# An MLP in two phases: the up projection by seven block products too, with its split outputs kept in DRAM between the phases

## The chip, the cores and the metric

The kernel runs on one core of a Trainium2 chip. The metric is device time in microseconds (us) of one launch. The kernel before takes 3120.62 us (median of 3 runs, 3118.38 to 3122.58). One profiled execution of it has a span of 3119.9 us.

## The reference

A decoder trunk of two layers over 1024 tokens of width 1024, all in float32. Layer 0 mixes by GLA linear attention and an RG-LRU, layer 1 by a gated DeltaNet. Each layer then attends to 256 memory tokens with 4 heads and applies an MLP of width 4096 with a squared ReLU. What the change touches:

```python
def sq_relu_mlp(h, w1, w2):
    return jnp.square(jax.nn.relu(h @ w1)) @ w2

def mem_cross_attn(h, mem_n, w_q, w_kv, w_o):
    q = (h @ w_q).reshape(B, T, XA_HEADS, XA_DH).astype(F32)
    kv = mem_n @ w_kv
    k = kv[..., :D_MODEL].reshape(B, M, XA_HEADS, XA_DH).astype(F32)
    v = kv[..., D_MODEL:].reshape(B, M, XA_HEADS, XA_DH).astype(F32)
    ...
```

`h` is the residual after an RMSNorm with gain. x is 1024 tokens by 1024, w1 is 1024 by 4096, w2 is 4096 by 1024.

## The kernel before

**Precision.** A float32 product is made from three fast ones. Each operand X is split into a high part (ScalarE copies it to the type fp32r, `whi`) and a low part (VectorE subtracts, `wlo`). TensorE then adds high*high, high*low and low*high into one PSUM bank. So every 128x128 block of weights costs three matmuls for each 512 tokens.

**Tiles.** Channels lie on the partitions, tokens in the free dimension, in halves of 512. The residual `hres` takes 32 KB of each partition, the split activations `act` 64 KB. Weights stream from DRAM in blocks of 512 KB through four slots (`wraw`, `whi`, `wlo`), in the order of the list that the host makes. SyncE (SP) issues these loads in that order, each after a wait until its slot is free. Each engine's instructions stand in an order written out by hand and run in that order. Semaphores tie the engines together. `plan` (functions `schedule` and `Plan`) only counts blocks and units and says which PSUM bank a unit uses and which unit must have been evacuated before.

**The MLP.** The 32 tiles of hidden channels are worked in 8 groups of 4. A group has an up projection (192 matmuls of 128x512: 4 tiles, 2 halves of the tokens, 8 tiles of the width, 3 products) and a down projection whose outputs VectorE adds to `work` (lines L1856 and L1989). In groups 0 and 7 the down projection has 192 matmuls too. In groups 1 to 6 (a hardware loop, `body(g)`) it has 168: for each of four blocks of W2 (a to d), taken as a 2x2 matrix of blocks A, and the hidden values, taken as a 2x2 matrix B (two tile pairs by two halves of the tokens), Strassen's method in Winograd's form makes seven block products in place of eight. `SUM` names the operands of each: product 1 is A11*B11, 2 is A12*B21, 3 is S4*B22, 4 is A22*T4, 5 is S1*T1, 6 is S2*T2, 7 is S3*T3. S1 to S4 are sums of blocks of A, T1 to T4 of B. `PRODUCTS` is their order: "a5" is product 5 of block a. VectorE makes the sums of the weights (L1909 to L1914) and of the hidden values (L1951 to L1976), ScalarE and VectorE split them (L1024 to L1040, L1925, L1926, L1946). TensorE's products are L2905 to L2907.

**Elsewhere.** The memory's keys and values are 16 units of 256 columns each. The values come out transposed and TensorE turns them (`value_transposes`). In the GLA stretch TensorE makes seven levels of 128x128 score blocks per chunk (L2961), VectorE selects from each with a mask (L2246, `select`), and GpSimd makes the decays (L640 to L666). At the start ScalarE issues the loads of x and then loads its table.

## Time and profile before

| | |
|---|---|
| median of 3 runs | 3120.62 us |
| span of the profiled execution | 3119.9 us |
| TensorE busy | 3059.8 us, 98% |
| VectorE busy | 1951.3 us, 63% |
| ScalarE busy | 1209.0 us, 39% |
| GpSimd busy | 165.4 us, 5% |
| DMA | 206.01 MB, mean 66 GB/s |

The profiled execution's own time is its span to within what the page shows; nothing else of that execution is timed. PE is TensorE, DVE VectorE, ACT ScalarE, POOL GpSimd, SP SyncE, and SPq or ACTq their issuing of DMAs. Busy time of an engine is time in which it executes, so overlapping matmuls count once. The duration of one matmul is longer than its share of the time, since the next one enters behind it; a rate is therefore read from starts, or from a window's length and its count. `L1234` is a line of the kernel.

### The profile page before, as it was taken

To read this page: it belongs to the slowest core of one execution; us is meant where nothing else is said; L and a number is where in the kernel's file an instruction comes from. 1 tells how busy PE (TensorE), PEld (TensorE's weight loads), DVE (VectorE), ACT (ScalarE), POOL (GpSimd) and SP (SyncE) were. 2 spreads that over 40 slices of the span, in tenths; PEclk is the share of its full clock that TensorE was granted. 3 is DMA by queue.
4 is the path that set the end of the run, shared out by engine and by line. 5 is a ranking of instruction groups with operands and counts; after the bars stand their busy time and mean duration, and the time that the engine had idled before them with its cause. 6 is when DMAs were issued, how large, how long until landed. Compare 5 with 4: busy or idle time off the path is not lost.

```text
span 3119.9 us, 46630 instructions
## 1 busy us (share of the span) xinstructions
PE 3059.8 (98%) x17630; PEld 2520.8 (81%) x17630; DVE 1951.3 (63%) x3087; ACT 1209.0 (39%) x2304; POOL 165.4 (5%) x270
## 2 busy tenths in 40 slices
PE   8999999999999999999999999999999999999997
PEld 6788898887888888887888788879888788888886
DVE  7276647547566666667555566644764756666666
ACT  3335545345332332244111366644534533333322
POOL 0019300000000000000000112100000000000000
PEclk9999999999999999999999999999999999999999
DMA  3110331012111111212222221123101211111122
GB/s 133 34 48 22 115 115 41 28 41 95 48 54 54 54 54 47 94 54 82 102 94 97 82 76 57 54 65 112 41 28 41 95 48 54 54 54 54 48 94 80
DMA packets 81321, 206.01 MB, mean 66 GB/s; under 512 B 6304, under 2 KB 39344, under 8 KB 80176
## 3 DMA queue, kind: packets, MB, share of 16 engines
q1 hardware_dynamic: 40320, 141.91, 14.0%
q10 hardware_dynamic: 40880, 62.41, 5.5%
q8 instruction: 85, 1.39, 0.2%
q14 instruction: 36, 0.29, 0.0%
HBM read 174.93 MB, written 29.36 MB: 65 GB/s over the span
## 4 chain that ended last, share of the span: by engine, by line
PE 86%; DVE 8%; ACT 3%; issue 2%; DMA 1%; ACTq 0%; DVEq 0%; SPq 0%
PE ps L2636 42%; PE ps L2652 14%; PE ps L2907 5%; PE ps L2905 5%; PE ps L2906 5%; PE ps L3071 2%; PE ps L3001 2%; DVE work L1545 1%; PE ps L3203 1%; PE ps L3076 1%; PE ps L2961 1%; DVE work L1561 1%; DVE hres L1576 1%; PE ps L3186 1%; DVE wlo L1529 1%
## 5 line engine op out<-in xcount | busy, mean ns | idle before, releaser
L2636 PE MATMUL ps<-act,whi 128*128 128x512 f32 x3664 | 1147.4, 394 | 6.7 <-DVE work L1706 2.7
L2636 PEld LDWEIGHTS ps<-act,whi 128*128 128x128 f32 x3664 | 684.3, 188 | 167.1 <-issue 12.2
L2636 PE MATMUL ps<-act,wlo 128*128 128x512 f32 x1832 | 717.1, 391 | 0.0
L1529 DVE TENSOR_TENSOR wlo<-wraw,whi 128x1024 fp32r<-128x1024 f32 x257 | 314.0, 1223 | 304.3 <-ACT whi L725 301.4
L725 ACT ACTIVATE whi<-wraw 128x1024 fp32r<-128x1024 f32 x214 | 225.5, 1056 | 570.4 <-DMA wraw<-wstream_dram 567.7
L2636 PEld LDWEIGHTS ps<-act,wlo 128*128 128x128 f32 x1832 | 343.9, 188 | 75.5
L2652 PE MATMUL ps<-act,whi 128*128 128x512 f32 x1376 | 370.7, 391 | 0.7 <-DVE work L2147 0.7
L2652 PEld LDWEIGHTS ps<-act,whi 128*128 128x128 f32 x1376 | 258.9, 188 | 57.0 <-issue 1.8
L1989 DVE TENSOR_TENSOR work<-work,ps 128x512 f32<-128x512 f32 x336 | 225.0, 684 | 103.8 <-PE ps L2907 103.8
L2652 PE MATMUL ps<-act,wlo 128*128 128x512 f32 x688 | 213.5, 391 | 0.0
L979 ACT ACTIVATE hidf<-hidf 128x512 f32<-128x512 f32 x96 | 60.8, 633 | 263.1 <-DVE hidf L1893 263.1
L2636 PE MATMUL ps<-hid,whi 128*128 128x512 f32 x512 | 160.2, 394 | 1.1 <-DVE hidf L1841 0.7
L2652 PEld LDWEIGHTS ps<-act,wlo 128*128 128x128 f32 x688 | 129.5, 188 | 27.8
L1018 ACT ACTIVATE whi<-wraw 128x1024 fp32r<-128x1024 f32 x48 | 49.2, 1049 | 186.8 <-DVE wraw L1910 186.8
L2636 PEld LDWEIGHTS ps<-hid,whi 128*128 128x128 f32 x512 | 95.9, 188 | 24.0 <-issue 2.1
L2905 PE MATMUL ps<-hid,whi 128*128 128x512 f32 x288 | 113.7, 395 | 0.0
L2907 PE MATMUL ps<-hid,wlo 128*128 128x512 f32 x288 | 113.3, 393 | 0.0
L1606 DVE SCALAR_TENSOR_TENSOR work<-work,pvec 128x1023 f32<-128x1023 f32 (+2 forms) x84 | 107.8, 1283 | 8.0 <-DVE work L1602 0.2
L2906 PE MATMUL ps<-hid,whi 128*128 128x512 f32 x288 | 112.7, 391 | 0.0
L671 POOL TENSOR_TENSOR work<-work,consts 128x512 f32<-128x512 f32 x16 | 20.4, 1273 | 1539.0 <-ACT work L1332 1539.0
L1893 DVE SCALAR_TENSOR_TENSOR hidf<-ps,work 128x512 f32<-128x512 f32 x96 | 66.2, 689 | 55.0 <-PE ps L2636 55.0
L2636 PE MATMUL ps<-hid,wlo 128*128 128x512 f32 x256 | 99.9, 390 | 0.0
(364 smaller groups left out, 4990.8 us busy)
## 6 DMA issues: line engine op xcount, KB each, us to landing
wraw<-wstream_dram SPq DMA_DIRECT2D x262, 512.0 KB, 3.6
qkvz<-work ACTq DMA_DIRECT2D x32, 512.0 KB, 2.7
work<-qkvz ACTq DMA_DIRECT2D x64, 256.0 KB, 3.3
hsave<-hres ACTq DMA_DIRECT2D x2, 4096.0 KB, 12.0
hres<-hsave ACTq DMA_DIRECT2D x2, 4096.0 KB, 12.8
hres<-xT_dram ACTq DMA_DIRECT2D x8, 512.0 KB, 11.0
hres<-xT_dram ACTq DMA_DIRECT2D x1, 4096.0 KB, 13.4
outT_dram<-hres SPq DMA_DIRECT2D x16, 256.0 KB, 2.0
```

The source lines that it names most:

```text
L725: A(whi[s][:], wraw[s][:], ACT.Copy).then_inc(w_hi, 1)
L1529: TT(wlo[s][:], wraw[s][:], whi[s][:].bitcast(F32), ALU.subtract).then_inc(w_split, 1)
L1606: ins = STT(out=out[:, back:], in0=x[:, 0:SEQ - back], scalar=w(3 - back), in1=out[:, back:], op0=ALU.mult, op1=ALU.add)
L1893: STT(out=hidf[:, t, 1, E[e]], in0=out_of(u + k), scalar=0.0, in1=uh(RSTD, e), op0=ALU.max, op1=ALU.mult).then_inc(evac, 1)
L1989: TT(uh(t, e), uh(t, e), out_of(u + 8 + i), ALU.add).then_inc(evac, 1)
L2636: last = mm(out_of(u)[:, 0:width], (wlo if hl else whi)[s][:, at:at + P], rhs(kt, xp, e), start=kt == hl == xp == 0, stop=kt == kts - 1 an ...
L2652: last = mm(out_of(u)[:, E[e]], (wlo if hl else whi)[s][:, kt * P:(kt + 1) * P], act[:, kt, xp, E[e]], start=kt == hl == xp == 0, stop=kt ...
L2905: mm(out_of(u), wh, bh, start=first, stop=False, skip_group_check=more)
L2906: mm(out_of(u), wh, bl, start=False, stop=False, skip_group_check=more)
L2907: last = mm(out_of(u), wl, bh, start=False, stop=end, skip_group_check=more)
L3001: last = mm(out_of(u), (wlo if hl else whi)[s][:, kt * P:(kt + 1) * P], act[:, kt, xp, E[c % 2]], start=kt == hl == xp == 0, stop=kt == KT ...
L3071: last = mm(out[:, (h % 4) * P:(h % 4 + 1) * P], lhs[:, h, :], rhs[:, h, :], start=start, stop=stop)
```

## The change

Both MLPs are worked in two phases.

**Up phase.** Group 0 is made as before. Group 1's up projection is made as before, but ScalarE evacuates it. The hidden tiles of groups 2 to 7 are made two at a time, in 12 pairs (`PAIRS`). For each pair the input x is the 2x2 matrix B (halves of the width by halves of the tokens) and the two weight blocks are A. The seven products of a pair, in the order 1, 5, 6, 2, 7, 3, 4, each have 12 matmuls. Products share PSUM banks: 1, 6, 7 and 4 accumulate into one bank, and ScalarE (`kept`) and VectorE (`corner`) read it between them. The four "quads" of a pair (two tiles by two halves) then get ReLU and square on ScalarE. GpSimd makes their sums T1 to T4 (`hidden_sums`), ScalarE the high parts (`part_hi`), VectorE the low ones (`part_lo`), and SP stores all seven split operands to DRAM (`store` to `hid_store`, 512 KB each). Group 0's hidden values go to `hid_first`. The norm's factor is left out of the hidden values of groups 1 to 7.

**Down phase.** Groups 1 to 7 are worked by seven products each, with operands read back from `hid_store` (`operand`) into the space of `act`, `tx` and `hres`, two groups alternating. Then GpSimd multiplies the sum by the square of the norm's factor and group 0 is added (192 matmuls).

**Engines.** The sums of the weights and of the hidden values go from VectorE to GpSimd (`weight_sums`, `hidden_sums`). All loads and stores of the MLP are issued by SP. The hardware loops over groups are gone: the program is written out.

**Elsewhere.** The memory's values are made with the memory as the stationary operand, in four full banks (96 matmuls of 512 columns for a layer, and no transposes). In the GLA stretch the seven levels are made and selected for half of the columns only. At the start SP issues the loads of x, tile 0 and the first halves of two weight blocks first, and ScalarE loads its table at once.

The core of the diff:

```diff
+UP = "1562734"
+STAGED = ("B11", "B22", "T1", "T3", "B21", "T2", "T4")
+LO_ORDER = ("B11", "B22", "B21", "T13", "T2", "T4")
...
+        for q in range(PAIRS):
+            blocks = [plan.block(ring[2 * (q % 2) + k]) for k in range(2)]
+            banks = {"1": 0, "6": 0, "7": 0, "4": 0, "5": 1, "3": 1, "2": 2}
+            for name in UP:
+                u = plan.fixed((0 if q % 2 else 4) + banks[name])
+                if name in "24":
+                    plan.after[blocks["24".index(name)]] = u
+            plan.by_hand.update(blocks)
+        here(f"mlp{layer}.d")
...
+                def store(hp, *ops):
+                    for op in ops:
+                        nth = LO_ORDER.index(op if op not in ("T1", "T3") else "T13")
+                        sp.wait_ge(hid_ready, HIDS * layer + 2 * MLP_T + len(LO_ORDER) * hp + nth + 1)
+                        sp.dma_start(hid_store[hp // 2, STAGED.index(op), :, hp % 2], stage(op).bitcast(F32)).then_inc(out_of_op(op), 16)
...
+                for q in range(PAIRS):
+                    last = q == PAIRS - 1
+                    if last:
+                        for op in ("B11", "T1", "T2"):
+                            operand(0, op)
+                    load(n + 2 * q + 4)
+                    if last:
+                        operand(0, "B21")
+                    store(q + 2, "B11", "B22")
+                    if last:
+                        operand(0, "T3")
+                        operand(0, "B22")
+                    load(n + 2 * q + 5)
+                    if last:
+                        operand(0, "T4")
+                    store(q + 2, "B21", "T1", "T3", "T2", "T4")
...
+                order = ("B11", "T1", "T2", "B21", "T3", "B22", "T4")
+                for op in order:
+                    operand(1, op)
+                n = plan.at[f"mlp{layer}.d"][0]
+                    load(n + MLP_T * i + 4)
+                    load(n + MLP_T * i + 5)
+                    more = i + 2 < MLP_G - 1
+                    for op in order:
+                        if op == "T2":
+                            load(n + MLP_T * i + 6)
+                        if more:
+                            operand(i + 2, op)
+                    load(n + MLP_T * i + 7)
...
+                def hidden_sums(hp):
+                    at = HIDDEN * layer + hp
+                    pool.wait_ge(squared, 4 * at + 3)
+                    if hp == 0:
+                        pool.wait_ge(first_out, 32 * (layer + 1))
+                    if hp:
+                        pool.wait_ge(*all_out("T1", layer, hp))
+                    tt(stage_part("T13", 1, True), quads[:, hp % 2, 1:3, :], quads[:, hp % 2, 0:2, :], ALU.subtract) \
+                        .then_inc(t_raw, 1)
+                    pool.wait_ge(t_raw, 3 * at + 1)
+                    tt(stage_part("T2", 1, True), quad(hp, "22"), stage_part("T1", 1, True), ALU.subtract).then_inc(t_raw, 1)
+                    pool.wait_ge(squared, 4 * at + 4)
+                    pool.wait_ge(t_raw, 3 * at + 2)
+                    tt(stage_part("T4", 1, True), quad(hp, "21"), stage_part("T2", 1, True), ALU.subtract).then_inc(t_raw, 1)
...
+                    k3 = link.mark(tt(s3, a11, a21, ALU.subtract))
+                    tt(a21, a21, a22, ALU.add).then_inc(w_sum, 1)
+                    link.wait(k3)
+                    k2 = link.mark(tt(s2, a22, s3, ALU.subtract))
+                    link.wait(k2)
+                    tt(s4, a12, s2, ALU.subtract).then_inc(x_sum, 1)
...
+                def kept(q, product, name):
+                    hp = q + 2
+                    uq = up_unit(layer, q, product)
+                    eng.wait_ge(t_raw, 3 * (HIDDEN * layer + hp - 1))
+                    eng.wait_ge(hid_ready, HIDS * layer + 2 * MLP_T + len(LO_ORDER) * (hp - 2) + 3)
+                    eng.wait_ge(unit_done, uq + 1)
+                    A(quad(hp, name), out_of(uq), ACT.Copy).then_inc(read_act, 1)
+                def corner(q, name):
+                    hp = q + 2
+                    eng.wait_ge(read_dve, 3 * (PAIRS * layer + q) + ("11", "22", "12").index(name) + 1)
+                    link(A(quad(hp, name), quad(hp, name), ACT.Relu))
+                    squares(hp, name)
...
+                for q in range(PAIRS):
+                    more = q + 1 < PAIRS
+                    if q:
+                        last_corner(q - 1)
+                    else:
+                        first_up(7)
+                    part_hi(q + 1, "B21")
+                    part_hi(q + 1, "T13")
+                    kept(q, "1", "11")
+                    part_hi(q + 1, "T2")
+                    if more:
+                        block_hi(blocks_of(layer, q + 1)[0])
+                    kept(q, "5", "22")
+                    part_hi(q + 1, "T4")
+                    if more:
+                        block_hi(blocks_of(layer, q + 1)[1], prep_no(layer, q + 1))
+                    else:
+                        down_hi(0, 0)
+                    kept(q, "6", "12")
+                    if more:
+                        sums_hi(prep_no(layer, q + 1), sums_of(q + 1))
+                    else:
+                        down_hi(0, 1)
+                    corner(q, "11")
+                    part_hi(q + 2, "B11")
+                    corner(q, "22")
+                    part_hi(q + 2, "B22")
+                    corner(q, "12")
+                last_corner(PAIRS - 1)
+                for op in LO_ORDER[2:]:
+                    part_hi(PAIRS + 1, op)
...
+                def part_lo(hp, op):
+                    at = HIDDEN * layer + hp
+                    eng.wait_ge(hid_hi, h0 + 2 * MLP_T + len(LO_ORDER) * hp + LO_ORDER.index(op) + 1)
+                    if op in ("T13", "T2"):
+                        eng.wait_ge(t_raw, 3 * at + (2 if op == "T13" else 3))
+                    src = stage_part(op, 1, True) if op[0] == "T" else quad(hp, op[1:])
+                    TT(stage_part(op, 1), src, stage_part(op, 0).bitcast(F32), ALU.subtract).then_inc(hid_ready, 1)
...
+                def corner(q, product, name):
+                    nth = ("11", "22", "12").index(name)
+                    eng.wait_ge(unit_done, up_unit(layer, q, product) + 1)
+                    eng.wait_ge(read_act, 3 * (PAIRS * layer + q) + nth + 1)
+                    TT(quad(q + 2, name), quad(q + 2, name), out_of(up_unit(layer, q, product)), ALU.add).then_inc(read_dve, 1)
...
+                for q in range(PAIRS):
+                    more = q + 1 < PAIRS
+                    x, bufs = prep_no(layer, q + 1), sums_of(q + 1)
+                    for op in LO_ORDER[2:]:
+                        part_lo(q + 1, op)
+                    if more:
+                        block_lo(blocks_of(layer, q + 1)[0], x)
+                    corner(q, "2", "11")
+                    if more:
+                        block_lo(blocks_of(layer, q + 1)[1], x)
+                    else:
+                        down_lo(0, 0)
+                    part_lo(q + 2, "B11")
+                    corner(q, "7", "22")
+                    if more:
+                        part_of_sums_lo(x, bufs, 0, "24")
+                    part_lo(q + 2, "B22")
+                    corner(q, "3", "12")
+                    if more:
+                        part_of_sums_lo(x, bufs, 1, "3")
+                    else:
+                        down_lo(0, 1)
+                def add(i, k):
+                    name = PRODUCTS[k]
...
+                for q in range(PAIRS):
+                    b0, b1 = blocks_of(layer, q)
+                    x, reads = prep_no(layer, q), 3 * (PAIRS * layer + q)
+                    for name in UP:
+                        u = up_unit(layer, q, name)
+                        if name in "152":
+                            eng.wait_ge(evac, plan.need[u] + 1)
+                        if name in "15":
+                            eng.wait_ge(w_split, (b0 if name == "1" else b1) + 1)
+                        if name in "67":
+                            eng.wait_ge(read_act, reads + (1 if name == "6" else 3))
+                            eng.wait_ge(x_split, 2 * x + (1 if name == "6" else 2))
+                        if name == "4":
+                            eng.wait_ge(read_dve, reads + 2)
+                        if q == 0 and name in "5674":
+                            eng.wait_ge(xt_ready, 8 * layer + 2 * "5674".index(name) + 2)
+                        a, op = SUM[name]
                         for k in range(4):
+                            last = multiply(out_of(u), weights(a, k, q), [moving(op, hl, k) for hl in range(2)],
+                                            k == 0 and name in "152", k == 3, name in "6734")
...
+                        if level < DIAG:
+                            half = CH >> (level + 1)
+                            new = at4.rearrange("p (a b) (n s t) -> p a (b n) s t", a=2, s=2, t=half)[:, :, :, 1, :]
+                            data = data.rearrange("p a (b s t) -> p a b s t", s=2, t=half)[:, :, :, 1, :]
+                            mask = masks[:, level, :].rearrange("p (b t) -> p b t", t=half).unsqueeze(1) \
+                                .to_broadcast(list(new.shape))
+                        else:
...
+                        for xp, hl in ((0, 0), (0, 1), (1, 0)):
+                            for k in range(2):
+                                last = mm(bank(4 + 2 * m + k), memhl[:, xp, at:at + P], (wlo if hl else whi)[s][:, E[k]],
+                                          start=kt == hl == xp == 0, stop=kt == KT - 1 and xp == 1)
+                    last.then_inc(unit_done, 1)
...
+            first_part(0, False)
+            for n in range(2):
+                first_hi(n, 0)
+            first_square(tile(hres, 0), 0)```

VectorE, in the middle of the up phase, one pair. `staged` is a low part that goes to DRAM, `wlo` that of a weight block, `xl_u` that of a weight sum, `quads<-quads,ps` is `corner`:

```order
547 L2229 TENSOR_TENSOR staged_78<-quads,staged_78 128x512 [waits hid_hi]
548 L2229 TENSOR_TENSOR staged_77<-stagedf_79,staged_77 128x2x512 [waits t_raw,hid_hi]
549 L2229 TENSOR_TENSOR staged_78<-stagedf_80,staged_78 128x512 [waits t_raw,hid_hi]
550 L2229 TENSOR_TENSOR staged_78<-stagedf_80,staged_78 128x512 [waits hid_hi]
551 L1871 TENSOR_TENSOR wlo_60<-wraw_56,whi_52 128x1024 [waits w_hi,x_sum]
552 L2236 TENSOR_TENSOR quads<-quads,ps 128x512 [waits read_act,unit_done]
553 L1871 TENSOR_TENSOR wlo_61<-wraw_57,whi_53 128x1024 [waits w_hi,x_sum]
554 L2229 TENSOR_TENSOR staged_77<-quads,staged_77 128x512 [waits hid_hi]
555 L2236 TENSOR_TENSOR quads<-quads,ps 128x512 [waits read_act,unit_done]
556 L2251 TENSOR_TENSOR xl_u_95<-xr_u_93,xh_u_91 128x1024 [waits x_hi]
557 L2229 TENSOR_TENSOR staged_77<-quads,staged_77 128x512 [waits hid_hi]
558 L2236 TENSOR_TENSOR quads<-quads,ps 128x512 [waits read_act,unit_done]
```

Nothing of this stood there before. The first read of PSUM (552) stands behind the low part of the next pair's weight block (551), which waits for `x_sum`.

GpSimd, in the same place, one pair. `stagedf` are T1 and T3, T2 and T4 of the hidden values, `xr_u` and `wraw` the sums of the weights:

```order
231 L871 TENSOR_TENSOR stagedf_79<-quads 128x2x512 [waits late_out,squared]
232 L874 TENSOR_TENSOR stagedf_80<-quads,stagedf_79 128x512 [waits t_raw]
233 L877 TENSOR_TENSOR stagedf_80<-quads,stagedf_80 128x512 [waits t_raw,squared]
234 L889 TENSOR_TENSOR xr_u_100<-wraw_58,wraw_59 128x512 [waits w_in3,w_in2]
235 L890 TENSOR_TENSOR wraw_59<-wraw_59 128x512
```

Before, GpSimd had no instruction in either MLP. `x_sum` is signalled by the second of two more instructions of this form behind 235.

SP, from the last pair into the first group of the down phase. `wraw` is a load of a weight block, the others read operands of the hidden values back:

```order
203 L744 DMA act<-hid_store 128x4x512 [waits early_out,unit_done]
204 L747 DMA act<-hid_store 128x2x512 [waits late_out,unit_done]
205 L747 DMA hresr<-hid_store 128x2x512
206 L695 DMA wraw_59<-wstream_dram 128x1024 [waits unit_done]
207 L695 DMA wraw_56<-wstream_dram 128x1024 [waits unit_done]
208 L695 DMA wraw_57<-wstream_dram 128x1024 [waits unit_done]
209 L744 DMA act<-hid_store 128x4x512 [waits early_out,unit_done]
210 L747 DMA tx<-hid_store 128x2x512 [waits late_out,unit_done]
```

Before, only weight blocks stood in this queue. Now each block stands behind operands that were issued ahead of it.

## Rows read from the trace of the kernel before

**Rows 1.** The page: busy time by engine, and the chain's shares.

```profile
PE 3059.8 (98%) x17630; PEld 2520.8 (81%) x17630; DVE 1951.3 (63%) x3087; ACT 1209.0 (39%) x2304; POOL 165.4 (5%) x270
...
PE 86%; DVE 8%; ACT 3%; issue 2%; DMA 1%; ACTq 0%; DVEq 0%; SPq 0%
```

**Rows 2.** Windows of two loop groups (up, down, up): length, busy (instructions), clock, DMA.

```profile
967.26:1011.38 44.12, 44.12 (x194) 36.24 (x193) 27.62 (x45) 18.29 (x28) 0.00 (x0) 1.00 0.20 71
1011.38:1049.93 38.55, 38.55 (x168) 31.35 (x167) 29.70 (x48) 7.86 (x12) 0.00 (x0) 1.00 0.08 27
1049.93:1094.04 44.11, 44.11 (x194) 36.24 (x193) 27.61 (x45) 18.29 (x28) 0.00 (x0) 1.00 0.22 71
```

**Rows 3.** VectorE groups: shapes, count, busy us, mean ns, idle before.

```profile
L1529 DVE TENSOR_TENSOR wlo<-wraw,whi 128x1024 fp32r<-128x1024 f32 x257 | 314.0, 1223 | 304.3 <-ACT whi L725 301.4 <-DVE work L1606 1.1
L1932 DVE TENSOR_TENSOR hid<-hidf,hid 128x512 fp32r<-128x512 f32 x72 | 49.3, 685 | 0.0
L1926 DVE TENSOR_TENSOR xl<-xr,xh 128x256 fp32r<-128x256 f32 x48 | 20.1, 419 | 0.0
```

**Rows 4.** ScalarE groups, same columns.

```profile
L725 ACT ACTIVATE whi<-wraw 128x1024 fp32r<-128x1024 f32 x214 | 225.5, 1056 | 570.4 <-DMA wraw<-wstream_dram 567.7 <-issue 2.6
L979 ACT ACTIVATE hidf<-hidf 128x512 f32<-128x512 f32 x96 | 60.8, 633 | 263.1 <-DVE hidf L1893 263.1
```

**Rows 5.** GpSimd groups, same columns.

```profile
L673 POOL TENSOR_TENSOR work<-work 128x512 f32<-128x512 f32 x16 | 20.3, 1270 | 93.3 <-PE ps L3154 93.3
L650 POOL TENSOR_TENSOR wlo<-wraw,whi 128x1024 fp32r<-128x1024 f32 x5 | 11.9, 2381 | 3.3 <-ACT whi L725 3.3
L666 POOL TENSOR_TENSOR lin<-lin,work 128x256 f32<-128x256 f32 x8 | 5.9, 735 | 0.0
```

**Rows 6.** Timeline, VectorE and GpSimd at 338 us: start, length, instruction.

```profile
337.85 2.38 POOL L650 TENSOR_TENSOR wlo<-wraw,whi 128x1024 fp32r<-128x1024 f32 x1 [1.97 <-ACT whi L725]
338.99 4.61 DVE L2296 TENSOR_TENSOR work<-work 128x512 f32<-128x512 f32 x2
340.19 2.86 POOL L701 TENSOR_TENSOR act<-work,act 128x1024 fp32r<-128x1024 f32 x1
```

**Rows 7.** Line L2296: ns min/median/max, first and last start.

```profile
L2296 DVE TENSOR_TENSOR work<-work x8: 678/684/2894, 339.0 to 349.8; 128x512 f32<-128x512 f32 x8
```

**Rows 8.** Timeline of PE: 256-column units of the memory; levels of the GLA stretch.

```profile
395.29 0.28 PE L2636 MATMUL ps<-memhl,wlo 128*128 128x256 f32 x1
395.41 0.40 PE L2636 MATMUL ps<-memhl,whi 128*128 128x256 f32 x2
395.64 0.28 PE L2636 MATMUL ps<-memhl,wlo 128*128 128x256 f32 x1
...
256.24 2.06 PE L2961 MATMUL ps<-lin 64*128 64x128 f32 x32
258.22 0.49 PE L2980 MATMUL ps<-lin 128*128 128x128 f32 x2
258.55 0.39 PE L2981 MATMUL ps<-lin 128*128 128x128 f32 x2
258.77 0.39 PE L2980 MATMUL ps<-lin 128*128 128x128 f32 x2
```

**Rows 9.** Window of the GLA stretch, columns as in Rows 2.

```profile
234.00:338.00 104.00, 102.76 (x870) 82.96 (x871) 70.43 (x117) 60.51 (x112) 92.75 (x192) 1.00 0.08 25
```

**Rows 10.** Timeline, the start.

```profile
7.59 1.28 ACT L1490 ACT_TABLE_LOAD   x1 [7.59 <-issue]
12.52 2.07 PE L2665 MATMUL ps<-act,whi 128*128 128x512 f32 x4 [12.52 <-DVE act L1589]
```

**Rows 11.** The page: DMA queues (packets, MB, share of 16 engines) and issues (to landing).

```profile
q1 hardware_dynamic: 40320, 141.91, 14.0%
q10 hardware_dynamic: 40880, 62.41, 5.5%
...
wraw<-wstream_dram SPq DMA_DIRECT2D x262, 512.0 KB, 3.6
...
hres<-hsave ACTq DMA_DIRECT2D x2, 4096.0 KB, 12.8
```

1051 lines of the change are left out of this document (577 added, 474 removed).

## The prediction

> **What bounds the kernel now.** I read the busy line and the chain first: TensorE is busy 98% of the span and the chain is 86% TensorE [rows 1]. Then the windows of two loop groups of the MLP: TensorE is busy for the whole of each, at full granted clock, while ScalarE and VectorE have room and GpSimd does nothing [rows 2]. So before the change only fewer or cheaper matmuls shorten the MLP, and the question for after is whether some other engine's order of work now takes longer than TensorE's. The last views are therefore durations by form [rows 3 to 5] and places where GpSimd and VectorE ran at once [rows 6, 7].
>
> The sum is made against the profiled execution. Its span, 3119.9 us, is 0.7 us under the median, 3120.6; I add the sum to the median. Two kernels of this time that differ by less than 0.2% (6 us) can't be told apart.
>
> **What goes on TensorE.** A down window has 168 matmuls in 38.55 us, 0.2295 us each, an up window 44.12 us [rows 2]. A pair in the new up phase has 84 matmuls, 19.3 us, so two pairs take 38.6 in place of 44.1: 5.5 us for each of 6 groups, 33 us. One more group's down projection gets seven products: 5.5 us. That is 38.7 us a layer, **-77.4 us**.
>
> Values of the memory: a layer drops 192 matmuls of 256 columns, three of which start in 0.35 us [rows 8], so 22.5 us, and 16 transposes. I price a transpose by the nearest 128-column matmuls, four in 0.44 us [rows 8], so 1.8 us. It adds 96 of 512 columns, 22.0 us. **-5 us** for both layers. Bounds: 0 (if the new order waits once for the blocks) and -8.
>
> GLA stretch: 32 level matmuls take 2.06 us [rows 8], 0.064 each; 56 of the 64 in each of 8 chunks lose half their columns, at most 14 us. But GpSimd, whose decays are not touched, is busy 92.75 of these 104 us [rows 9], which leaves at most 11. At the other end the load of weights sets the pace and nothing is gained. I take **-6 us**, the middle. Start: the first matmul is at 12.52 us, the table load at 7.59 behind the issuing of the loads of x [rows 10]. If the table is loaded at once and x tile 0 comes first, up to 8 us go; if the stream of x tiles then paces TensorE, none. **-4 us**.
>
> Sum of what goes: -92 us.
>
> **Up phase, a steady pair.** GpSimd now makes the sums. A 512-element sum takes 1.27 us (L673 in [rows 5]), back to back 1.25; a 1024-element one 2.38 (L650 in [rows 5]). One pair: T1 and T3 together 2.4, T2, T4 and four weight sums 6 x 1.25, in all 9.9 us. VectorE: two weight blocks and a 1024 weight sum, 1.14 each back to back, a 512 one 0.6, the staged low parts 5 x 0.6 and 1.14, in all about 8.1 us, all with both inputs in SBUF, and three reads of PSUM (2 us). ScalarE: about 14 us from its two forms, 1.06 and 0.63 [rows 4]. Each alone fits into 19.3.
>
> They don't run freely beside each other. At 338 us L2296, with both inputs in SBUF and 0.684 us alone, took 2.89 us at the longest [rows 7]: two of them took 4.61 us while two GpSimd instructions ran, each VectorE one ending just after a GpSimd one did, and GpSimd's second took 2.86 in place of 2.4 [rows 6]. So such an instruction waits for the whole of GpSimd's running one, and GpSimd for it. The Trainium skill, page "SBUF — State Buffer", section "Who interferes with whom", states this as a rule: a VectorE instruction with two SBUF inputs and a GpSimd one that reads SBUF exclude each other, and whichever began first keeps the port. It speaks against this change; by it the whole 18 us of both would stand in one row in every pair, and the trace agrees where the two met.
>
> The loop of waits of one pair, from the start of GpSimd's T1/T3 sum (0). GpSimd: 2.4; VectorE's low part of B21, which has waited, 0.6; T2 1.25; T4 1.25; VectorE's T1/T3 low part 1.1; first weight sum 1.25; VectorE's T2 part 0.6; second weight sum 1.25 (at 9.7); VectorE's T4 part 0.6; the last two weight sums 2.5: x_sum at 12.8. Only then may VectorE make the low part of the weight block, 1.2, and behind it in its queue read product 2's bank, 0.7. ScalarE: ReLU, square, high part of B11, 1.9. VectorE: low part of B11, then product 7's bank, 1.4 (this releases product 4 on TensorE). ScalarE the same again, 1.9; VectorE low part of B22 and product 3's bank, 1.4; ScalarE ReLU and square, 1.3. With that the last quad is ready and GpSimd starts the next pair: 9.9 us after x_sum with the short hops between. The loop is 22.65 us against TensorE's 19.3, and TensorE then waits about 3.35 us a pair, before products 7 (ScalarE's read of product 6 stands behind the second weight block, which waits for the second sum) and 4.
>
> Eleven such steps, 37 us. Ahead of them the same exclusion and the 8 sums of the inputs (8 x 2.4) delay ScalarE's queue in group 1's up projection, so that the first pair's loop starts up to 9 us late; I take 4. The last pair ends 1 us late. 42 us a layer, **+84 us**. Bounds: 11 (no exclusion, below) and 125 (both engines' 18 us in one row and nothing hidden: the loop grows by 1.7 more).
>
> **Into the down phase.** DMA: queue q1 moved 141.91 MB in 14.0% of the span, 325 GB/s, q10 62.41 MB in 5.5%, 364 [rows 11]. An operand pair of a group is 1 MB, a group 7.3 MB, about 21 us. Operands of group 1 of the phase may only be loaded as the last pair frees the space, and T4's last: it lands about 11 us after the pair's end, product a6 wants it at 8.3: 3 us. SP then issues the late stores of the last pair (2.6 MB) and seven operands of the next group (7.3 MB) ahead of the next group's first weight block. That block lands about 40 us into the group, but VectorE's queue wants its low part behind the 20th addition, at 31; TensorE runs out of banks at product d6. 11 us. **+28 us** for both layers; bounds 0 and 40.
>
> In a steady down group VectorE has 28 additions from PSUM (17 us back to back, not excluded) and 8 us of splits, GpSimd 16 sums of 256 elements (0.735 each [rows 5], 12 us) in 38.6 us: hidden by TensorE. The 9.4 MB of a group are 29 us at 325 GB/s: hidden. The 16 multiplications of the end take 20 us beside 44 us of TensorE. More instructions because loops are written out: nothing, since issuing is 2% of the chain [rows 1] (bounds -2 and +10).
>
> **The sum.** -92 + 84 + 28 = +20: 3141 us, with its own range 3115 to 3168.
>
> **Rivals.** One, not slower, and much faster: exclusion does not decide. VectorE's four staged parts (2.85 us) then run beside GpSimd and the loop is 19.8 us, 0.5 over TensorE: 11 us in all, and the late start goes. With 22 us into the down phase: 3120.6 - 92 + 33 = 3062. For it: only two instructions of full size met GpSimd in this trace. Against it: both waited. It decides wherever the loop is under about 20.5 us a pair. Chance 0.22.
>
> Two: exclusion holds, but late start and transition are hidden, because loads run ahead of my count: 3120.6 - 92 + 74 = 3103. For it: the block of 512 KB lands in 3.6 us [rows 11] and each wait is short when the queue is empty. Chance 0.15.
>
> Three: the round trip through DRAM decides. A pair moves 4.7 MB (14.5 us at 325 GB/s, 22 at 215), a group 9.4. If reading and writing in pieces of 2 KB came to 215 GB/s, a down group would take 44 us in place of 38.6: 5 x 6 x 2 = 60 more, 3200. Against it: q10, the queue with the smaller packets, is not the slower one [rows 11]. Chance 0.08.
>
> **Numbers.** The forecast has 0.55, rivals 0.22, 0.15 and 0.08. Faster by over 0.2%: rivals one and two and a corner of the forecast, 0.38. Within 0.2%: the forecast's lower edge and two's upper, 0.11. Slower: 0.51. The range must reach both sides: 3062 to 3170 leaves out rival three and half of what lies below one.
>
> **What would show it.** In the up phase windows of one pair of about 22.6 us with 84 matmuls; VectorE's lines L2229 and L1871 with durations well over 0.69 and 1.22, up to 3 us, and GpSimd's sums over 1.27; TensorE waiting for ScalarE's `kept` ahead of product 7 and for VectorE's `corner` ahead of 4. One gap of some 10 us in the first down group, behind a wait on `x_sum`. Steady down groups of 38.6 us. First matmul near 8 us. I am wrong if the pairs take 19.3 to 20 us, or if VectorE's durations don't stretch where GpSimd runs.

## The result and the profile after

The changed kernel takes 3213.7 us (median of 4 runs, 3210.2 to 3221.3) against 3120.5 before (3118.4 to 3122.6): ratio 1.030, 95% interval 1.029 to 1.031. The forecast, 3141, had the sign and not the size; the time is outside its range. The profiled execution has a span of 3211.8 us, 91.9 more than that of before.

The page of the changed kernel, busy line and shares of the chain, for [rows 1]:

```profile
PE 3031.0 (94%) x17070; PEld 2453.7 (76%) x17070; DVE 1970.8 (61%) x2817; ACT 1390.8 (43%) x2556; POOL 768.6 (24%) x722
...
PE 59%; DVE 11%; POOL 11%; ACT 7%; issue 5%; DMA 5%; SPq 0%; ACTq 0%; DVEq 0%; POOLq 0%
```

TensorE has 560 matmuls less and is the chain for 59% in place of 86%: it now waits for others. Windows show where: one pair of the up phase, down groups 2, 4 and 1 (for [rows 2]). A row has the window, its length, the busy time (instructions) of TensorE, its weight loads, VectorE, ScalarE and GpSimd, the granted clock, the DMA engines' share and GB/s.

```profile
855.55:878.20 22.65, 20.20 (x85) 15.55 (x84) 12.68 (x14) 14.29 (x21) 12.27 (x7) 1.00 0.56 209
1144.75:1183.90 39.15, 39.15 (x169) 31.39 (x168) 27.35 (x40) 6.00 (x9) 9.02 (x12) 1.00 0.58 206
1224.97:1266.72 41.75, 39.26 (x169) 31.38 (x168) 28.49 (x40) 8.00 (x12) 12.94 (x16) 1.00 0.64 228
1089.13:1144.75 55.62, 43.98 (x167) 34.84 (x168) 30.73 (x43) 12.74 (x19) 17.77 (x22) 0.85 0.93 341
```

A pair takes 22.65 us, a down group 39 to 44, the first one of layer 0 55.6 at a granted clock of 0.85 (that of layer 1 took 57.3). Durations by form, for [rows 3, 5]:

```profile
L2229 DVE TENSOR_TENSOR staged<-stagedf,staged 128x512 fp32r<-128x512 f32 x56 | 86.3, 1577 | 30.5 <-POOL stagedf L877 30.5
L2251 DVE TENSOR_TENSOR xl_u<-xr_u,xh_u 128x1024 fp32r<-128x1024 f32 x24 | 29.2, 1217 | 0.0
```
```profile
L871 POOL TENSOR_TENSOR stagedf<-quads 128x1024 f32<-128x1024 f32 x28 | 74.5, 2660 | 257.1 <-ACTq L1275 257.1
L877 POOL TENSOR_TENSOR stagedf<-quads,stagedf 128x512 f32<-128x512 f32 x28 | 61.8, 2205 | 4.0
L892 POOL TENSOR_TENSOR xr_u<-wraw,xr_u 128x512 f32<-128x512 f32 x24 | 41.2, 1719 | 0.0
```

A 512-element VectorE subtraction, 0.685 us alone, takes 1.58 where GpSimd works beside it; the split of the sums, made while GpSimd is idle, keeps its 1.22. GpSimd's 512-element ones take 1.7 and 2.2 in the mean of these two groups, in place of 1.27.

The timeline of GpSimd in one pair shows the loop as the prediction drew it, for [rows 6]. A row has start, length and instruction, and in brackets the idle time before it and what ended it:

```profile
857.68 2.41 POOL L871 TENSOR_TENSOR stagedf<-quads 128x1024 f32<-128x1024 f32 x1 [10.11 <-ACTq L1275]
...
861.93 2.35 POOL L877 TENSOR_TENSOR stagedf<-quads,stagedf 128x512 f32<-128x512 f32 x1
...
868.96 1.28 POOL L894 TENSOR_TENSOR xr_u<-wraw,xr_u 128x512 f32<-128x512 f32 x1
880.36 2.41 POOL L871 TENSOR_TENSOR stagedf<-quads 128x1024 f32<-128x1024 f32 x1 [10.12 <-ACTq L1275]
```

From the first subtraction to the end of the last sum 12.6 us (forecast 12.8), then 10.1 idle (9.9): 22.7.

Where the 72 us between the forecast's 20 over before and the measured 92 lie, by differences of such windows over both layers:

| part | forecast | measured | short by |
|---|---|---|---|
| 24 pairs over TensorE's 19.3 each | 84 | 106 (steady 68, first pairs 19, last pairs 18) | 22 |
| first down groups over 38.55 | 28 | 36 | 8 |
| down groups 2 to 7 | 0 | 27 | 27 |
| entry of the up phase | 0 | 8 | 8 |
| everything outside the MLP (start, GLA stretch, memory values) | -15 | -8 | 7 |

### The profile page after: what moved, and what is told of

It is laid out like the page before. It is cut to its first block, busy times and chain, and to the rows that moved or that the text cites. A ratio compares the mean times of both kernels' runs of the same rounds, so it can differ in the third digit from the quotient of the medians.

```text
span 3211.8 us, 44831 instructions
## 1 busy us (share of the span) xinstructions
PE 3031.0 (94%) x17070; PEld 2453.7 (76%) x17070; DVE 1970.8 (61%) x2817; ACT 1390.8 (43%) x2556; POOL 768.6 (24%) x722
## 4 chain that ended last, share of the span: by engine, by line
PE 59%; DVE 11%; POOL 11%; ACT 7%; issue 5%; DMA 5%; SPq 0%; ACTq 0%; DVEq 0%; POOLq 0%
PE ps L2944 17%; PE ps L2960 14%; PE ps L3166 4%; PE ps L3167 4%; PE ps L3168 4%; DMA wraw<-wstream_dram 4%; POOL stagedf L871 2%; PE ps L3394 2%; POOL stagedf L877 2%; POOL wraw L890 2%; PE ps L3324 2%; DVE quads L2236 1%; ACT quads L1274 1%; PE ps L3016 1%; DVE work L1887 1%
## 5 line engine op out<-in xcount | busy, mean ns | idle before, releaser
L2944 PE MATMUL ps<-act,whi 128*128 128x512 f32 x2384 | 754.0, 397 | 10.7 <-DVE wlo L1871 5.2
L2944 PEld LDWEIGHTS ps<-act,whi 128*128 128x128 f32 x2384 | 445.6, 188 | 120.5 <-issue 13.1
L1871 DVE TENSOR_TENSOR wlo<-wraw,whi 128x1024 fp32r<-128x1024 f32 x255 | 319.1, 1253 | 254.5 <-ACT whi L985 173.3
L2960 PE MATMUL ps<-act,whi 128*128 128x512 f32 x1376 | 371.0, 391 | 0.7 <-DVE work L2434 0.7
L2319 DVE TENSOR_TENSOR work<-work,ps 128x512 f32<-128x512 f32 x360 | 242.6, 684 | 160.3 <-PE ps L3168 159.1
L2960 PEld LDWEIGHTS ps<-act,whi 128*128 128x128 f32 x1376 | 259.0, 188 | 57.0 <-issue 1.8
L3166 PE MATMUL ps<-act,whi 128*128 128x512 f32 x624 | 250.8, 402 | 30.9 <-DVE quads L2236 18.0
L916 POOL TENSOR_TENSOR hres<-hres 128x1024 f32<-128x1024 f32 x16 | 42.7, 2709 | 870.4 <-ACT hres L1250 870.4
L3166 PEld LDWEIGHTS ps<-act,whi 128*128 128x128 f32 x624 | 118.3, 190 | 71.3 <-DVE quads L2236 28.0
L3167 PE MATMUL ps<-act,whi 128*128 128x512 f32 x416 | 164.3, 395 | 0.0
L3167 PE MATMUL ps<-hresr,whi 128*128 128x512 f32 x416 | 163.8, 394 | 0.0
L2229 DVE TENSOR_TENSOR staged<-stagedf,staged 128x512 fp32r<-128x512 f32 (+1 forms) x84 | 122.7, 1486 | 60.4 <-POOL stagedf L877 30.5
L2229 DVE TENSOR_TENSOR staged<-quads,staged 128x512 fp32r<-128x512 f32 x84 | 72.7, 869 | 120.8 <-ACT staged L1298 120.8
## 6 DMA issues: line engine op xcount, KB each, us to landing
wraw<-wstream_dram SPq DMA_DIRECT2D x260, 512.0 KB, 3.5
hid_store<-staged SPq DMA_DIRECT2D x196, 512.0 KB, 3.1
hresr<-hid_store SPq DMA_DIRECT2D x56, 512.0 KB, 10.3
qkvz<-work ACTq DMA_DIRECT2D x32, 512.0 KB, 2.6
tx<-hid_store SPq DMA_DIRECT2D x28, 512.0 KB, 7.7
act<-hid_store SPq DMA_DIRECT2D x28, 512.0 KB, 11.2
```

The source lines that it names most:

```text
L1871: TT(wlo[s][:], wraw[s][:], whi[s][:].bitcast(F32), ALU.subtract).then_inc(w_split, 1)
L2229: TT(stage_part(op, 1), src, stage_part(op, 0).bitcast(F32), ALU.subtract).then_inc(hid_ready, 1)
L2319: TT(uh(t, e), uh(t, e), out_of(uk), ALU.add).then_inc(evac, 1)
L2944: last = mm(out_of(u)[:, 0:width], (wlo if hl else whi)[s][:, at:at + P], rhs(kt, xp, e), start=kt == hl == xp == 0, stop=kt == kts - 1 an ...
L2960: last = mm(out_of(u)[:, E[e]], (wlo if hl else whi)[s][:, kt * P:(kt + 1) * P], act[:, kt, xp, E[e]], start=kt == hl == xp == 0, stop=kt ...
L3166: mm(out, wh, xh, start=first, stop=False, skip_group_check=more)
```

## Experiments

**e1 and e5: the exclusion by itself.** Small kernels outside the model, stages of 16 instructions.

> Not the model at all: ten stages of 16 instructions each, one after the other, on idle memory. Alone (stage 1 and 2) a VectorE subtraction of two SBUF tiles of 512 should take about 0.6 us back to back and a GpSimd one 1.25 (as in the trace of before). Theory (the two exclude each other for whole instructions when both read two SBUF tiles): side by side (stage 3) they alternate, a pair of them every 1.85 us, 30 us for 16 pairs in place of 20. With VectorE's second input in PSUM (stage 4) or its only input in PSUM (stage 5), as in the additions of the down phase, nothing stretches: 10 and 20 us. Rival (bandwidth shared, no exclusion): stage 3 takes about 20 us for GpSimd and less than 20 for VectorE, and stages 4 and 5 stretch as much as stage 3. Stages 8 to 10 add ScalarE copies and eight loads of 512 KB: if DMA or ScalarE also stretch VectorE by over 5%, the loop of the up phase has a third cause.

> Not the model: nine stages of GpSimd fills, GpSimd copies and GpSimd subtractions, alone and beside VectorE's subtractions of two SBUF tiles. Theory (what VectorE shares with GpSimd is a way of reading SBUF): a fill on GpSimd, which reads nothing, leaves VectorE's 16 subtractions at 9.7 us, and a GpSimd copy, which reads one tile, stretches them as a subtraction does (over 17 us). Rival (any GpSimd instruction that touches SBUF holds VectorE up): the fills stretch them too. With 1024-element VectorE subtractions (8 of 1.15 us) beside GpSimd's, the total is again close to the sum of both. A fill's own time is wanted for the next experiment, where it takes the place of a sum.

Timelines of e1: VectorE alone, then beside GpSimd's subtractions with two SBUF inputs, with the second input in PSUM, with its only input in PSUM, and with its only input in SBUF (a copy). GpSimd's rows follow: alone, and in the first two of these stages.

```profile
9.25 9.72 DVE L392 TENSOR_TENSOR dout<-din 128x512 f32<-128x512 f32 x16 [4.11 <-DMA ain<-xT_dram]
38.84 25.70 DVE L392 TENSOR_TENSOR dout<-din 128x512 f32<-128x512 f32 x16 [19.87 <-POOL pout L367]
65.79 9.66 DVE L394 TENSOR_TENSOR dout<-din,ps 128x512 f32<-128x512 f32 x16 [1.25 <-POOL pout L367]
85.57 9.66 DVE L396 COPY dout<-ps 128x512 f32<-128x512 f32 x16 [10.13 <-POOL pout L367]
105.32 21.44 DVE L398 COPY dout<-din 128x512 f32<-128x512 f32 x16 [10.09 <-POOL pout L367]
...
19.15 19.56 POOL L367 TENSOR_TENSOR pout<-pin 128x512 f32<-128x512 f32 x16 [18.71 <-DVE dout L392]
38.88 26.78 POOL L367 TENSOR_TENSOR pout<-pin 128x512 f32<-128x512 f32 x16 [0.17 <-POOL pout L367]
65.83 19.61 POOL L367 TENSOR_TENSOR pout<-pin 128x512 f32<-128x512 f32 x16 [0.17 <-POOL pout L367]
```

Side by side, 16 of each take 26.8 us; the sum of both alone is 29.3, free overlap would be 19.6. With one input in PSUM nothing stretches. The eight loads and ScalarE's copies beside them changed nothing: VectorE took 25.75 us in that stage, and ScalarE's 16 copies 8.43 us there and in the stage with VectorE's PSUM input. In e5 VectorE's 16 took 9.72 us beside GpSimd fills and 15.9 beside GpSimd copies (expected over 17). So the exclusion stands, for GpSimd instructions that read, and is a little milder than whole instructions in one row: 9% less than the sum.

VectorE's SBUF-to-SBUF copies, with one SBUF input, stretched as well: 21.4 us beside GpSimd, where the same copies from PSUM took 9.66 (from SBUF they were not run alone). The Trainium skill, page "SBUF — State Buffer", section "Who interferes with whom", states the rule with this exception: two SBUF inputs contend with a GpSimd instruction that reads SBUF and not with one that only writes it; at most one SBUF input does not contend, outside modes with two ports, which a copy can enter; ScalarE never waits, and DMA does not contend with a compute engine. The stages agree with it.

**e2: the wait that the table names.**

```diff
+                    kept(q, "6", "12")
                     if more:
                         block_hi(blocks_of(layer, q + 1)[1], prep_no(layer, q + 1))
                     ...
-                    kept(q, "6", "12")
```

> ScalarE's read of product 6 stands ahead of the high part of the second weight block, which waits for GpSimd's second weight sum; nothing else moves. The waits of the changed kernel show 1.3 to 1.7 us a pair of TensorE ahead of product 7 for this read. Theory A (a loop through GpSimd's sums, VectorE's read of product 2 behind x_sum and ScalarE's queue sets the pair; this gap is only slack that the loop leaves): pairs stay at 22.6 us, the gap moves to product 4, total unchanged within 5 us. Rival B (each gap is its own cost): pairs of about 21.3 us, 24 of them, 30 us less.

3215.9 us, the same as the changed kernel within its spread; pairs of 24.3, 21.2 and 22.7 in turn, 22.7 in the mean. Theory A: the wait ahead of product 7 is gone, the one ahead of product 4 grew from 0.86 to 1.5 and 2.5 us, and the loop stayed. The forecast of pairs at 22.6 holds for their mean only.

**e3: the loop opened.** VectorE's order in a pair, condensed to names (ScalarE's was moved likewise, and in the last pair both engines' first splits for the down phase stand behind the pair; each kind of instruction keeps its own order):

```diff
-    part_lo B21, T13, T2, T4; block_lo 0; corner 2; block_lo 1; part_lo B11; corner 7; sums 24; part_lo B22; corner 3; sums 3
+    part_lo B21, T13, T2; corner 2; part_lo T4; corner 7; block_lo 0; part_lo B11; block_lo 1; corner 3; sums 24; part_lo B22; sums 3
```

> The same instructions in the up loop in another order: VectorE reads product 2 (and 7) ahead of the low parts of the weight blocks, which wait for x_sum, and ScalarE takes product 6 and the rectifying of product 2 ahead of the sums' high parts. GpSimd is untouched. Theory A (exclusion stretches a loop of waits that closes through x_sum; the engines have 18 us of excluded work for 19.3 us): with the read of product 2 out of the loop pairs fall from 22.65 to 19.3 to 20 us, 11 x 2 x 3 = 60 to 70 us less in all, though VectorE and GpSimd still wait for each other instruction by instruction. Rival B (the 18 us of both in one row are themselves the bound, or DMA is): the order gives little, pairs stay above 22, under 10 us less.

3146.5 us, 67 less; ratio to before 1.0076 (1.0059 to 1.0093). A window of one pair, and two of VectorE's rows in the next:

```profile
854.42:873.83 19.41, 19.41 (x85) 15.78 (x84) 16.35 (x14) 13.99 (x22) 12.24 (x7) 1.00 0.66 244
```
```profile
874.53 2.89 DVE L2250 TENSOR_TENSOR xl_u<-xr_u,xh_u 128x512 fp32r<-128x512 f32 x1
877.34 1.78 DVE L2228 TENSOR_TENSOR staged<-quads,staged 128x512 fp32r<-128x512 f32 x1
```

VectorE is busier than before the edit (16.35 us in place of 12.68: its instructions are stretched more) and TensorE no longer waits in a steady pair. The exclusion costs only where it lies in the loop. The first pairs (28.4 and 29.1 us) and the last ones (29.3 and 28.9) stayed.

**e4: SyncE's queue.** In each down group the four weight blocks are asked for ahead of the seven operands; in the transition two blocks go ahead of the last three operands.

```diff
-                        if op == "T2":
-                            load(n + MLP_T * i + 6)
-                        if more:
-                            operand(i + 2, op)
-                    load(n + MLP_T * i + 7)
+                    load(n + MLP_T * i + 6)
+                    load(n + MLP_T * i + 7)
+                    if i + 2 < MLP_G - 1:
+                        for op in order:
+                            operand(i + 2, op)
```

> Only the order of SyncE's queue in the down phase: in each group the four loads of the next weight blocks come ahead of the seven operands of the group after next, and in the transition two weight blocks go ahead of the last three operands. Theory A (weight blocks land late behind 7 MB of operands, so x_sum is late, VectorE's additions behind it stop and TensorE runs out of banks ahead of c6 in steady groups and d6 in the first): steady groups fall from 40.7 to about 38.7 and the first from 55.6 by 8 to 10 us, 30 to 45 us less in all. Rival B (GpSimd's sums excluding VectorE's splits make the stops): groups stay at 40.7 and the gain is under 10 us. Rival C (DMA as a whole is the bound, 9.4 MB a group): the gap moves to the group's start (operands), no gain.

3203.4 us, 10 less in place of 30 to 45. The first down groups took 46.5 and 49.6 us in place of 55.6 and 57.3, as expected; groups 2 to 6 took 41.5 in the mean, 40.9 without the edit, so neither A nor B held there as written: the stop went from c6 to d6 and d4. Another block now follows the operands: in group 4 GpSimd stood 18.9 us, to 1245.91, for a block.

**e6: each block when its slot comes free.** On top of e3: the operands stand on either side of two blocks (four, two blocks, three), and B21 ahead of T2.

> The new order of the up loop (3146.5 us) and another order on SyncE: each weight block is asked for as soon as its slot comes free, with the seven operands of the group after next split around two of them (four operands, two blocks, three operands, two blocks); in the transition operand B21 goes ahead of T2. Theory (blocks or operands that land late make every stop of the down phase): a6/c6/d6 stops go; the first down group falls from 56.8 and 57.5 to about 45, steady groups to 38.7 to 39.5; the last pair, whose 10 us are a wait for operand B21 behind 7 MB of stores and loads, falls by 3. In all 3146.5 - 22 - 16 - 6, about 3102. Rival (in steady groups GpSimd's sums and VectorE's splits exclude each other, and that makes the stops): steady groups stay at 40.7 and the total at about 3120.

3115.7 us, 31 less than e3 (expected 3102, the rival 3120). Windows of groups 2 and 3 of layer 0:

```profile
1143.92:1183.15 39.23, 39.23 (x170) 31.36 (x168) 27.60 (x40) 7.30 (x12) 10.39 (x15) 1.00 0.70 242
1183.15:1222.34 39.19, 39.19 (x169) 31.39 (x168) 27.37 (x40) 8.95 (x13) 13.46 (x19) 1.00 0.69 241
```

TensorE is busy throughout, with more bytes a second than in the changed kernel's group 4. So the stops of the steady groups came from blocks that landed late. Neither the bytes nor the exclusion makes them by itself, though the exclusion adds to them where a block is late. Groups 2 to 7 of both layers together were 26 us over 38.55 each in e3 and 12 in e6; 14 us is what the order of the queue is worth. The first down groups fell from 56.8 and 57.5 to 51.2 and not to 45: d6 waits 1.4 and 0.8 us, but a1 waits 7 and a6 6 us for their operands. The last pairs fell by 2.7.

**e7: first pair and last group.** `kept(0, "1")` ahead of `part_hi(1, "B21")`, and the last group's `down_lo(i, 3)` four additions earlier.

> The last version with two more moves: in the first pair ScalarE reads product 1 ahead of the parts of the next hidden pair (TensorE stood 7 us ahead of product 6 for this read, behind GpSimd's first subtraction of that pair, stretched to 4.9 us), and in the last down group VectorE takes the low parts of the fourth block's sums 4 additions earlier, ahead of GpSimd's final multiplications (two of them took 3.2 us beside those, and c6 waited). Theory: first pair falls by 5 to 7 us, last group by 2, so 14 to 18 us less than the version before. Rival (the first pair is held by the sums of the inputs, which GpSimd ends at 789 us and which exclude VectorE): the wait moves to product 7 and the total stays within 5 us.

3108.3 us, 7.4 less: first pairs 25.8 and 24.6 in place of 27.9 and 29.2, last groups 39.8 in place of 40.7. About half of what was expected; in layer 1 part of the first pair's wait (1.4 us) moved to product 7, as the rival had it. Ratio to before 0.9967 (0.9953 to 0.9981): 0.3% faster than the kernel before, small but clear of its interval.

**e8: the same order, no exclusion.**

```diff
-                    tt(stage_part("T4", 1, True), quad(hp, "21"), stage_part("T2", 1, True), ALU.subtract).then_inc(t_raw, 1)
+                    fill(stage_part("T4", 1, True), 2, 128).then_inc(t_raw, 1)
```

and the other six likewise, so this kernel leaves out the sums' values.

> The changed kernel in its own order; in the up phase GpSimd's seven subtractions of a pair (hidden differences and weight sums) are left out, and fills of the same tiles stand in their place, two whole ones and one of part of the tile each, with the same waits and signals, so that GpSimd is busy as long (0.47 us for a fill of 512, 1.2 to 1.4 us for what was a 512-element sum, 2.4 for the 1024-element one). Fills read no SBUF and did not stretch VectorE's subtractions when measured by themselves. The sums' values are left out of the computation. Theory (exclusion is what lengthens the loop): VectorE's staged parts and splits go back to 0.69 and 1.22 us, the loop falls from 22.65 to about 20 us a pair, 11 x 2 x 2.7 = 60 us less in all, though no instruction's place is changed. Rival (the loop is long by its order and the engines' own times, and exclusion only fills idle time): pairs stay above 22 us, under 15 us less.

3155.7 us, 58 less. One pair:

```profile
864.59:885.35 20.76, 19.90 (x85) 15.54 (x84) 10.61 (x15) 14.06 (x21) 9.60 (x21) 1.00 0.61 228
```

No instruction changed its place, and VectorE is busy 10.6 us in place of 12.7. About 1.9 of the 3.3 us a pair were exclusion; 1.4 us are the order itself (rival one had 0.5, at 19.8; from the first fill to the end of the last there were 10.6 us where it counted 9.9, and 10.1 behind them). The expected 60 us came in another way: 20 steady pairs gave 40, and the two first pairs 13 (21.6 and 23.1 us in place of 29.0). So most of the first pair's excess was exclusion too.

**e9: the last pair's queue.** Operands in the order in which their space comes free, then blocks, then the seven stores.

> The best version so far (3108.3 us) with SyncE's queue of the last pair in another order: the seven operands of the first down group in the order in which their space comes free, the blocks of that group behind product 3's and 4's, and the last pair's seven stores behind all of them. Theory (the 7 us ahead of a1 and the 7 to 9 ahead of a6 are operands queued behind 3.7 MB of stores and blocks): 3 us less ahead of a1 and 3 to 5 ahead of a6 in each layer, 12 to 16 us less, about 3095. Rival (the operands' own 7.3 MB, 21 us, decide, or the block that a5 to c1 want now comes late): the stops move to the block's first use or stay, under 5 us.

3108.3 us, no change; ratio to before 0.9961 (0.9949 to 0.9973). In layer 0 the wait ahead of a6 fell from 5.5 to 1.0 us, and in its place came 2.7 ahead of c6 and 1.8 ahead of d6: GpSimd's sums of the fourth block stood 11.9 us for the stores that were put back. The rival's number holds. Why is an estimate: two groups' operands (14.7 MB), the stores (3.7 MB) and four blocks (2.1 MB) are 20.5 MB, 53 us at the 390 GB/s of the windows there (e10, last column), and from the first of these operands' issue (1035 us) to the end of the busy stretch of the DMA engines (1088) it was 53 us. So the bytes themselves seem to be the limit there, whoever goes first; no run with fewer bytes tests it.

**e10: TensorE kept busy in a wait.**

```diff
+                                if i == 0:
+                                    for _ in range(26):
+                                        mm(out_of(u), weights("A11", 0, None, i, j)[0], whi[...][:, E[0]], start=True, stop=True)
                                 eng.wait_ge(first_ops_in[i % 2], 16 * 4 * nth)
```

> The version with both orders and the two moves (3108.3 us), with 26 matmuls of 512 columns added on TensorE in each layer ahead of its wait for the first down group's operands, into the bank that a1 then starts anew, so their results are dropped; at 0.23 us each they take 6.0 of the 6.9 us of that wait. In that version 12 and 7 matmuls behind this wait start 0.39 to 0.52 us apart in place of 0.23 (granted clock of 0.5), 2.5 and 1.5 us. Theory (TensorE's clock falls because it stood idle, and matmuls behind a long wait cost double for some us): with TensorE busy in the wait, a1 and a5 run at full clock and the group ends 1.5 to 2.5 us earlier in each layer, 3 to 5 us less in all. Rival (the clock falls for another reason, or what stops next, a6's operands, ends last anyway): total the same within 2 us, since a6 waits 5.5 us for its operands whatever comes before; then only the wait ahead of a6 grows by what a1 and a5 gain.

3113.1 us (3106.5 to 3119.0), no gain where 3 to 5 us less were expected. Windows of TensorE around the wait, with the added matmuls and without (e7):

```profile
1044.00:1048.00 4.00, 1.11 (x5) 0.77 (x5) 3.31 (x2) 3.88 (x8) 3.92 (x2) 0.97 1.02 389
1048.00:1052.00 4.00, 4.00 (x13) 3.14 (x12) 4.00 (x4) 3.03 (x5) 3.60 (x4) 0.61 1.05 390
1052.00:1056.00 4.00, 4.00 (x19) 3.32 (x18) 1.82 (x2) 2.00 (x3) 2.33 (x3) 1.00 1.06 305
```
```profile
1044.00:1048.00 4.00, 0.00 (x0) 0.00 (x0) 4.00 (x4) 3.77 (x8) 3.57 (x4) 0.79 1.04 390
1048.00:1052.00 4.00, 3.74 (x9) 3.00 (x10) 3.75 (x5) 1.81 (x3) 3.52 (x3) 0.50 1.07 355
1052.00:1056.00 4.00, 4.00 (x17) 3.19 (x16) 2.98 (x5) 0.57 (x2) 0.00 (x0) 0.86 1.01 307
```

The half clock now fell on the added matmuls (26 in 7.8 us, not 6.0, and begun 2.9 us into the wait), and a1 and a5 ran at full clock; the groups were 2.9 and 3.7 us shorter and the pairs ahead of them, which hold the added matmuls, 3.6 and 3.8 longer. That the clock falls where TensorE has stood still is borne out; that it can be had back this way is not.

## Why the prediction was right and wrong

**The steady pair: right.** Mechanism and place hold: 22.65 us forecast and measured, x_sum after 12.6 us for 12.8. e1, e5 and e8 show the exclusion, e3 the loop through product 2's read. That the total agrees to 0.1 us is in part luck: by e8 the exclusion is 1.9 us a pair and the order 1.4, where the prediction had 2.85 and 0.5. Rival one (3062, exclusion does not decide) is refuted by e8 against the changed kernel. The two small waits a pair on TensorE, 1.3 us ahead of product 7 and 0.9 ahead of 4, are where the prediction put them, and e2 shows that they are no causes. Rival two (start and transition hidden) is refuted by the first pairs and first groups below, rival three (215 GB/s decide) by e6, whose groups of the same bytes take 39.2 us, and by windows of 389 and 390 GB/s (e10).

**TensorE's products: right.** With the waits gone (e3) two pairs take 38.7 us in place of 44.1 [rows 2]. A down group without a stop takes 39.2 us (e6) and not 38.55, 8 us over the twelve.

**The first pair: mis-sized.** "I take 4", of bounds up to 9. It was 9.7 us a layer. TensorE's row ahead of product 6:

```profile
816.41 0.79 PE L3166 MATMUL ps<-tx,xh_u 128*128 128x512 f32 x1 [6.60 <-ACT quads L1307]
```

Product 1 was done at 807.0 us. ScalarE read it at 815.78, behind its splits of the inputs and group 1's last tiles (to 812.95) and behind a part that needs GpSimd's first subtraction of the pair, for which it stood 1.86 us:

```profile
809.83 4.89 POOL L871 TENSOR_TENSOR stagedf<-quads 128x1024 f32<-128x1024 f32 x1 [8.22 <-ACTq L1275]
814.81 1.06 ACT L1298 ACTIVATE staged<-stagedf 128x1024 fp32r<-128x1024 f32 x1 [1.86 <-POOL stagedf L871]
```

That subtraction ran 4.9 us, in place of 2.4, beside VectorE's splits of the inputs. The delay was known; which instruction was queued behind it was not looked up. e7 took part of it back, and e8, without the exclusion, most of it.

**The last pair: mis-sized.** "Ends 1 us late" was 10.1 and 8.3 us over 19.3, of which 3.35 were a steady pair's. In TensorE's rows it stood 2.4 us as in a steady pair, then 5.4 and 3.6 us for operands ahead of a1, at the entry of the down phase, which the prediction had only ahead of a6; some 1.5 more are matmuls at half clock:

```profile
1089.37 0.76 PE L3166 MATMUL ps<-act,whi 128*128 128x512 f32 x1 [5.36 <-DMA act<-hid_store]
1101.87 0.47 PE L3166 MATMUL ps<-tx,xh_d 128*128 128x512 f32 x1 [2.59 <-DVE xl_d L2251]
1136.12 0.77 PE L3166 MATMUL ps<-tx,xh_d 128*128 128x512 f32 x1 [8.82 <-DVE work L2317]
```

The last two rows are the 3 us ahead of a6 and the 11 ahead of d6 of the forecast, 2.6 and 8.8 (4.6 and 7.2 in layer 1). The forecast's reason for a6, operands that land late, is what ended the wait in layer 1; in layer 0 it was VectorE's low part of a weight sum. e4 showed the cause of d6's, the block behind the operands. The first groups as a whole were 36 us over in place of 28: the waits came to 11.4 and 11.8 us a layer for the forecast's 14, and about 5 us more a layer were matmuls at half clock, for which the sum had no term.

**Steady down groups: the step that failed.** "The 9.4 MB of a group are 29 us at 325 GB/s: hidden." As a sum that is true; e6 moves them in groups of 39.2 us with no wait. But SyncE's queue brings them in one burst, and the block wanted first is issued last. GpSimd and VectorE in group 4 (which begins at 1224.97):

```profile
1242.61 0.74 POOL L889 TENSOR_TENSOR xr_d<-wraw 128x256 f32<-128x256 f32 x1 [12.32 <-DMA wraw<-wstream_dram]
...
1245.60 1.74 DVE L1871 TENSOR_TENSOR wlo<-wraw,whi 128x1024 fp32r<-128x1024 f32 x1 [1.45 <-POOL xr_d L894]
...
1249.28 1.87 DVE L2319 TENSOR_TENSOR work<-work,ps 128x512 f32<-128x512 f32 x3
...
1250.10 0.47 PE L3166 MATMUL ps<-tx,xh_d 128*128 128x512 f32 x1 [2.49 <-DVE work L2319]
```

The block lands 17.6 us into the group, its sums take 2.9, VectorE stands for 1.45 and then needs 3.7 us for splits of 2.2 beside GpSimd's next sums; three additions are late, TensorE has no bank: 2.5 us. I had made this argument for the first group (40 us against 31) and not for the others, where the sum is ready at 20.6 us and VectorE's queue is there at 19.2. Groups 2 to 7 were 27 us over the forecast: TensorE stood 17 us in them, and most of the rest is the 39.2 us of a group without a stop. The order of the queue gives back 14 of it (e3 to e6). The other large part of the miss is the first and last pairs, 21 us. The 16 multiplications at the end were not hidden either, and there by the exclusion alone: beside them two splits took 3.2 us in place of 1.0 (e4's trace), and the last group ended 0.9 us later than with the splits moved ahead (e7).

**The entry of the up phase: missed.** TensorE waits for low parts of weight blocks 2.6 us ahead of group 1's up projection (at 756.86) and 1.4 us ahead of the first product (at 804.04), and likewise in layer 1; no part of the sum had it.

**The gains outside the MLP: half.** The memory's values gave 1.8 and 1.3 us in place of 5; layer 1's mixing ran 3.2 us shorter, which no term had and no run explains. GLA stretch, "the middle" of 0 and 11: 0.4. The 32 level matmuls of 64 columns, for [rows 8], and the start:

```profile
255.66 2.00 PE L3284 MATMUL ps<-lin 64*128 64x64 f32 x32
...
8.40 2.05 PE L2973 MATMUL ps<-act,whi 128*128 128x512 f32 x4 [8.40 <-DVE wlo L2883]
```

Half the columns took 2.00 us in place of 2.06; the price of a level matmul is not in its columns, and the halving by columns was the error. The first matmul came 4.1 us earlier, as taken; by 228 us 1.0 was left of it. The granted clock was 0.69 and 0.50 in the windows from 30 to 34 us, behind a wait of 1.96 us that was 1.37 before; in the kernel before it stayed at 1.00 there.

**Chances.** 0.08 for a time of about 3200 was too little. The three rivals were each one mechanism; what came was several small waits, in the transitions and in the steady down groups, all of one sign.

## What to carry to other kernels

Price an added load by when it lands against when its first user's queue reaches it, in every group and not as bytes over a group: here 9.4 MB a group, "hidden", cost 14 us more in one order of the queue than in another (e3 and e6). When a wait table names a wait in a loop, first look for the loop (what is late next if this is gone): e2 removed the named one for nothing, e3 the right one for 67 us. GpSimd work beside VectorE instructions with two SBUF inputs stretches both by nearly whole instructions (26.8 of 29.3 us in e1), but it costs time only if those lie in the loop that sets the pace.

## What the runs showed of the hardware

- Behind eleven waits of 2.0 to 8.8 us TensorE ran at half clock: 86 of the matmuls in the changed kernel's products start 0.38 to 0.52 us apart in place of 0.23, 17 us in all (61 and 12 us in e7). Nearly all come in runs of 5 to 13, 1 to 2.6 us each, behind waits in the first and last pairs and in the first down group, and once in group 5. The windows there have a granted clock of 0.50, the 1.2 GHz level (1089 to 1091 us, behind the 5.4 us ahead of a1), and 0.97 to 1.00 ahead of the wait; behind the waits of 1.3 us in the steady pairs, and that of 2.5 us in group 4, it stayed at 1.00. No term of the prediction had this. It is at most a fifth of the loss: in e10 a1 and a5 at full clock did not shorten the time.
- VectorE's and GpSimd's subtractions took 9% less than the sum of both when they alternated (26.8 of 29.3 us, e1).
- SyncE's issue of a 512 KB read of the hidden values took 0.52 us at least, 1.03 in the median of `hresr<-hid_store` and up to 3.8 where such reads were issued one behind the other; that of a 512 KB weight block took 0.33 in the median. A long burst delays not only its own transfers but also the moment at which SyncE comes to what follows.
